# A two-layer decoder step on one core: the first pass of the output projection stores its split weight tiles, the second pass loads them back

## What is computed

```python
def gated_out(o, gate, w_o):
    return (o * jax.nn.silu(gate)) @ w_o

mp = gated_out(o.reshape(n_b, seq, MLA_WIDTH), gate, mla_w_o[l])   # 2048 -> 1024
hp = hp + rmsnorm(mp, post_norm[i])
```

## Time and profile before

| | us |
|---|---|
| median of 3 runs | 1649.53 |
| lowest and highest | 1646.85, 1650.47 |
| the profiled execution | 1646.13 |
| its span | 1644.3 |
| TensorE busy in the span | 1573.4 |
| second pass, from its first matmul to the next stage's first | 73.95 |

### The profile page before, as it was taken

The page is one execution under the profiler, slowest core; times in us unless marked ns, Lnnn a source line. Parts: engine busy times, 40 slices in busy tenths (PEclk is TensorE's granted clock), DMA queues, the critical chain, the costliest instruction groups (busy, mean ns, idle before and its releaser), DMA issues.

```text
span 1644.3 us, 27925 instructions
## 1 busy us (share of the span) xinstructions
PE 1573.4 (96%) x10778; PEld 1481.1 (90%) x10778; DVE 843.6 (51%) x1488; ACT 573.8 (35%) x1250; POOL 619.7 (38%) x683
## 2 busy tenths in 40 slices
PE   7999999899999999999999889999899999999996
PEld 7999999799999999999999668999899999977895
DVE  5227411675766757575756454006974430179416
ACT  4113111344444444444444343012232220289421
POOL 2433334133333333333332523456623324279610
PEclk9999999999999999999999999999999999999998
DMA  4122233011111111111115964227344223354223
GB/s 182 51 64 86 94 99 114 33 43 52 49 43 51 44 42 46 52 46 40 46 57 176 339 247 167 75 66 244 123 176 166 102 76 127 129 155 139 78 100 119
DMA packets 96077, 170.13 MB, mean 103 GB/s; under 512 B 9826, under 2 KB 63859, under 8 KB 95667
## 3 DMA queue, kind: packets, MB, share of 16 engines
q1 hardware_dynamic: 84372, 130.97, 24.4%
q10 hardware_dynamic: 6208, 21.26, 3.2%
q0 software_dynamic: 5376, 16.26, 2.7%
HBM read 129.04 MB, written 41.50 MB: 104 GB/s over the span
## 4 chain that ended last, share of the span: by engine, by line
PE 85%; DVE 9%; issue 3%; ACT 2%; POOL 1%; DMA 0%; DVEq 0%; SPq 0%; ACTq 0%; POOLq 0%
PE ps L128 27%; PE ps L987 8%; PE ps L2291 6%; PE ps L1054 6%; PE ps L2495 6%; PE ps L1038 4%; PE ps L993 3%; PE ps L1000 2%; PE ps L1018 2%; PE ps L1019 2%; PE ps L1020 2%; PE ps L1021 2%; PE ps L1022 2%; PE ps L2421 2%; PE ps L2897 1%
## 5 line engine op out<-in xcount | busy, mean ns | idle before, releaser
L683 POOL TENSOR_SCALAR b_prob<-b_prob,b_share 128x896 f32<-128x896 f32 (+7 forms) x128 | 97.3, 761 | 280.2 <-DVE b_share L903 278.9
L1946 POOL CAST w_hi_d<-w_raw_d 128x1024 fp32r<-128x1024 f32 x38 | 44.6, 1173 | 231.4 <-PE ps L128 109.3
L128 PE MATMUL ps<-a_xh,w_hi_a 128*128 128x344 f32 x552 | 119.6, 326 | 11.2 <-DVE a_xl L398 11.2
L781 ACT ACTIVATE b_pth<-ps 128x512 fp32r<-128x512 f32 (+1 forms) x160 | 86.2, 555 | 99.8 <-PE ps L1038 90.9
L128 PE MATMUL ps<-a_xl,w_hi_a 128*128 128x344 f32 x552 | 118.4, 323 | 0.0
L128 PE MATMUL ps<-a_xh,w_lo_a 128*128 128x344 f32 x552 | 118.0, 323 | 0.0
L773 ACT ACTIVATE b_prob<-ps,b_least 128x896 f32<-128x896 f32 (+7 forms) x128 | 94.8, 743 | 50.6 <-DVE b_least L895 49.5
L908 DVE TENSOR_TENSOR b_ptl<-ps,b_pth 128x512 fp32r<-128x512 f32 (+1 forms) x160 | 99.1, 632 | 24.7 <-ACT b_pth L781 23.6
L895 DVE TENSOR_REDUCE b_least<-ps 128x1 f32<-128x896 f32 (+7 forms) x128 | 96.2, 752 | 30.1 <-PE ps L1024 29.4
L128 PEld LDWEIGHTS ps<-a_xh,w_hi_a 128*128 128x128 f32 x552 | 94.2, 191 | 12.1 <-issue 11.6
L987 PE MATMUL ps<-cqh,b_w_hi 128*128 128x344 f32 x300 | 99.3, 331 | 0.2 <-DVE b_ql L835 0.2
(11 more groups left out here) (369 smaller groups left out, 4509.8 us busy)
## 6 DMA issues: line engine op xcount, KB each, us to landing
w_raw_d<-in_w_tiles SPq DMA_DIRECT2D x46, 512.0 KB, 3.6
c_pages<-in_cache_pages SPq DMA_DIRECT2D x80, 160.0 KB, 3.7
w_raw_a<-in_w_tiles SPq DMA_DIRECT2D x23, 512.0 KB, 3.5
gate_scratch<-a_stage ACTq DMA_DIRECT2D x16, 512.0 KB, 2.6
o_scratch<-b_ov POOLq DMA_DIRECT2D x64, 128.0 KB, 2.6
q_scratch<-f_qst ACTq DMA_DIRECT2D x16, 512.0 KB, 3.6
s_q<-q_scratch SPq DMA_DIRECT2D x32, 256.0 KB, 4.0
b_gate<-gate_scratch SPq DMA_DIRECT2D x60, 128.0 KB, 2.7
```

The lines of the kernel that those rows point to most:

```text
L128: mm = nc.tensor.matmul(ps[:, bank + c, 0:CH], wt, xt[:, k0 + k, c * CH:(c + 1) * CH], start=first and x == 0, stop=last and x == 2)
L683: nc.gpsimd.tensor_scalar(prob[:, n % 4, 0:keys], prob[:, n % 4, 0:keys], share[:, n % 4:n % 4 + 1], 1.0, ALU.mult, ALU.mult).then_inc(nor ...
L781: nc.scalar.activation(pth[:, n % 4, 0:cols], ps[:, 4 + n % 2, 0:cols], ACT.Copy).then_inc(pt_hi, 1)
```

## The change

After a tile of the first pass is split, SyncE stores its high and low part in a scratch tensor in HBM (`split_dram`, 16 tiles of 2 x 512 KB). The second pass loads the parts of its tiles from there (`load_again`) and splits nothing: neither GpSimd nor VectorE works on tiles 16 to 31. It uses four places, the fourth being the space of the two raw tiles (`of_raw`). The extra raw tiles `raw_more` are gone. The stores of tiles 0 and 1 are in `mla_samples`, behind the early heads' loads and the raw loads and ahead of `wv`. GpSimd now waits, before it writes over a split tile of the first pass, until that tile's store is complete (`split_kept`). The semaphores for stores and loads are ones that earlier loads of cache pages used, so counts start at a base.

```diff
@@ mla_samples, sync
         load_tile(nc, sp, w, a["w_tiles"], B_MO, 1, 0)
+        for u in range(2):
+            sp.wait_ge(w.split, u + 1)
+            for i, part in enumerate((w.hi, w.lo)):
+                nc.sync.dma_start(g.split_dram[1 - u, i], part[:, u, :].bitcast(F32)).then_inc(page_in[0][u], 16)
         sp.wait_ge(scored, ROUNDS * CHUNKS)
@@ out_and_swa_front
+    of_raw = at("w_of_raw_d", [P, 2, D], 66048, R32)
+    fourth = of_raw[:, 0, :], of_raw[:, 1, :]
-    raw_more = at("m_raw_more", [P, 2, D], 156672)
-    by_dve = [t for t in range(N_OUT, first_f) if t % 2]
-    slot = [(t - N_OUT + 2) % 3 if N_OUT <= t < first_f else t % 2 for t in range(n_tiles)]
+    slot = [t % 2 if t not in again else 2 if t == first_f - 1 else (2, 0, 1, 3)[t % 4] for t in range(n_tiles)]
...
+    def split_again(eng, t):
+
+        eng.wait_ge(split_in[slot[t]], split_in_base[slot[t]] + 32 * sum(slot[b] == slot[t] for b in range(N_OUT, t + 1)))
+
+    def split_kept(eng, t):
+
+        eng.wait_ge(split_out[t % 2], split_out_base[t % 2] + 32 * (t // 2 + 1))
@@ sync
+        def keep_split(t):
+            split_done(sp, t)
+            for i, part in enumerate(parts(t)):
+                nc.sync.dma_start(g.split_dram[t, i], part.bitcast(F32)).then_inc(split_out[t % 2], 16)
+
+        def load_again(t):
+            if slot_before[t] is not None:
+                sp.wait_ge(w.used, slot_before[t] + 1)
+                if slot_before[t] < N_OUT:
+                    split_kept(sp, slot_before[t])
+            elif slot[t] == 2:
+                sp.wait_ge(w.used, N_OUT - 1)
+            else:
+                split_done(sp, N_OUT - 1)
+            kept = t - N_OUT
+            split_kept(sp, 1 - kept if kept < 2 else kept)
+            for i, part in enumerate(parts(t)):
+                nc.sync.dma_start(part.bitcast(F32), shaped(g.split_dram[kept, i], t)).then_inc(split_in[slot[t]], 16)
+
+        for t in range(3, N_OUT):
             load(t)
-        sp.wait_ge(w.used, N_OUT)
+            keep_split(t - 1)
+        keep_split(N_OUT - 1)
+        for t in (N_OUT, N_OUT + 1, N_OUT + 3, N_OUT + 2):
+            load_again(t)
         for k in range(KT):
             nc.sync.dma_start(x_early[:, k, :], a["x_turned"][k][:, 0:SPLIT]).then_inc(x_early_in, 16)
-        for t in range(N_OUT + 3, N_OUT + 6):
-            load(t)
+        for t in range(N_OUT + 4, N_OUT + 8):
+            load_again(t)
         for k in range(KT):
             nc.sync.dma_start(x_late[:, k, :], a["x_turned"][k][:, SPLIT:TOK]).then_inc(x_late_in, 16)
-        for t in range(N_OUT + 6, first_f + 2):
-            load(t)
+        for t in range(N_OUT + 8, first_f - 4):
+            load_again(t)
+        for t in range(first_f - 4, first_f - 1):
+            load_again(t)
+        sp.wait_ge(w.used, first_f - 4)
+        load(first_f), load(first_f + 1)
+        load_again(first_f - 1)
@@ gpsimd
+                if t < N_OUT:
+                    split_kept(pool, t - 2)
...
-        for t in range(2, n_tiles):
+        for t in [t for t in range(2, n_tiles) if t not in again]:
@@ vector: the eight calls rest(17), rest(19), ... rest(31) are gone, for instance
-        rest(21)
         to_unit(0, 2), add_x(0, 2), x_low(0, 1)
@@ tensor, second pass
         for t in range(N_OUT, first_f):
             j = t // 2 - KT
-            split_done(pe, t)
+            split_again(pe, t)
```

More of the change, by code:

```diff
@@ L1682, in mla_samples @@
     p.sync, p.gpsimd, p.scalar, p.vector, p.tensor = sync, gpsimd, scalar, vector, tensor
+    p.pages_landed = [(landed, 16 * 4 * (QUAD - len(by_pool))) for landed, by_pool in zip(page_in[0], pool_share)]
     p.own_made, p.clear_queries, p.find_pages, p.load_query_weights = own_made, clear_queries, find_pages, load_query_weights
@@ L1852, in out_and_swa_front, with split_number, raw_before @@
     v_order = (NT,) + tuple(range(NT))
-    by_dve = [t for t in range(N_OUT, first_f) if t % 2]
+    again = range(N_OUT, first_f)
     v_tiles = (n_tiles - 2, n_tiles - 1)
[L1855 to L1858, removed]
-    slot = [(t - N_OUT + 2) % 3 if N_OUT <= t < first_f else t % 2 for t in range(n_tiles)]
+    slot = [t % 2 if t not in again else 2 if t == first_f - 1 else (2, 0, 1, 3)[t % 4] for t in range(n_tiles)]
     slot_before = [max((b for b in range(t) if slot[b] == slot[t] and b not in v_tiles), default=None) for t in range(n_tiles)]
-    def raw_tile(t):
-        return w.raw[:, raw_slot[t], :] if raw_slot[t] < 2 else raw_more[:, raw_slot[t] - 2, :]
+    def split_number(t):
+        return t + 1 if t < N_OUT else t + 1 - N_OUT
+    def raw_before(t):
+        return t - 2 if t != first_f and t != first_f + 1 else t - 2 - N_OUT
     def parts(t):
@@ L1871, in parts @@
             return w.hi[:, slot[t], :], w.lo[:, slot[t], :]
-        return third
+        return third if slot[t] == 2 else fourth
     def parts_of(t, k):
@@ L1889, in split_done @@
     def split_done(eng, t):
[L1891 to L1894, removed]
+        eng.wait_ge(w.split, split_number(t))
+    def split_again(eng, t):
+        eng.wait_ge(split_in[slot[t]], split_in_base[slot[t]] + 32 * sum(slot[b] == slot[t] for b in range(N_OUT, t + 1)))
+    def split_kept(eng, t):
+        eng.wait_ge(split_out[t % 2], split_out_base[t % 2] + 32 * (t // 2 + 1))
     def sync(sp, swa_samples):
@@ L1898, in load @@
             n = t - first_f
[L1899 to L1903, removed]
+            tile = B_MO + t if t < first_f else B_SIN + (n if n < NQ + 2 else n + 2 if t not in v_tiles else n - NQ)
@@ new lines, in load @@
+            split_done(sp, raw_before(t))
+            nc.sync.dma_start(w.raw[:, t % 2, :], a["w_tiles"][tile]).then_inc(w.landed[t % 2], 16)
+        def keep_split(t):
[15 more added lines that the diff above has]
+                nc.sync.dma_start(part.bitcast(F32), shaped(g.split_dram[kept, i], t)).then_inc(split_in[slot[t]], 16)
@@ L1938, in split @@
             hi, lo = parts(t)
-            pool.wait_ge(landed[raw_slot[t]], 16 * raw_count[t])
+            pool.wait_ge(w.landed[t % 2], 16 * ((t if t < N_OUT else t - N_OUT) // 2 + 1))
             if t in v_tiles:
@@ L1944, in split @@
             else:
[L1945 to L1949, removed]
-        for t in range(2, n_tiles):
+                pool.wait_ge(w.used, slot_before[t] + 1)
+                if t < N_OUT:
+                    split_kept(pool, t - 2)
+            nc.gpsimd.tensor_copy(hi, w.raw[:, t % 2, :]).then_inc(w.rounded, 1)
+            pool.wait_ge(w.rounded, split_number(t))
+            nc.gpsimd.tensor_tensor(lo, w.raw[:, t % 2, :], hi.bitcast(F32), ALU.subtract).then_inc(w.split, 1)
+        for t in [t for t in range(2, n_tiles) if t not in again]:
             if t == clear_at:
@@ L2147, in add_late @@
                                     ALU.add).then_inc(summed_late, 1)
-        def rest(t):
-            hi, lo = parts(t)
-            dve.wait_ge(w.rounded, t + 1)
-            nc.vector.tensor_tensor(lo, shaped(raw_tile(t), t), hi.bitcast(F32), ALU.subtract).then_inc(split_dve, 1)
         def spaces(of, to, n, root_sem, root_no, inv_sem, space_sem):
```

11 lines of the change are left out of this document (3 added, 8 removed).

## The result

The changed kernel takes 1638.83 us (median of 11 runs, 1633.98 to 1640.19), the kernel before, measured beside it, 1646.85 us (11 runs, 1642.11 to 1650.47). The ratio is 0.994, with a 95% interval of 0.993 to 0.9951: 8 to 11.5 us less. The forecast was 1639 and -10.2 us. The profiled execution took 1640.03 us for a span of 1638.3.

A forecast was written before the change was run, and what follows sets the result against it. TensorE bounds the kernel, held up in the second pass by VectorE's late splits; -10.9 - 0.3 + 1.0 = -10.2 us, from a median of 1649.53 to 1639. Gain range 7 to 13 us; 8 in 10 between 1634 and 1647.

The forecast's parts named there:

- -10.9 in the second pass: Second pass of the output projection: 73.95 us would fall to 63.0 once tiles 16 to 31 need no splitting.
- first two parts: Second pass's lost 10.9 us: about 5.2 are TensorE's waits for late low parts, 3.1 half speed after them.
- The remaining 2.6 are many waits of a few tenths: Second pass: the last 2.6 of the 10.9 us lost were put down to short TensorE waits at tile starts.
- VectorE left with 44 us, 37 without the slowdown: Second pass: VectorE's 64.25 us less 20 for eight subtractions leaves at most 44, 7 less without mutual slowdown.
- they lengthen each other's work: Second pass: VectorE and GpSimd slow each other; a low part takes 0.93 us with GpSimd resting, else 1.85.
- Neither can be late on its own account.: Second pass: without the splits, VectorE and ScalarE (21 us) are both paced by TensorE.
- -0.3 behind the pass: Behind the second pass: the second column sum no longer waits for VectorE's last additions, gaining 0.3 us.
- +1.0 for the DMA: Second pass: reload waits, likeliest at tiles 20 and 24, put between 0 and 2.9 us and taken as 1.
- The stores: 32 stores of 512 KB: cost 0 in the first pass; those of tiles 0 and 1 at most 1 us.
- 352 GB/s: Rival 1, second pass: reload at this rate instead of 407, gain 5.3 to 8.3 us, about 1642.5; chance 0.16.
- Rival 2: Second pass: third place loads at only 154 GB/s, 6.8 us a tile; net +5 us, 1654.5; chance 0.06.
- Rival 3: No change: VectorE or ScalarE sets the pace, or store waits cost the first pass; 1648 to 1650; chance 0.08.

## Why the prediction was right

- **-10.9 in the second pass.** Measured -10.46 (73.95 to 63.49), and -10.2 to -10.5 in the part that all profiles share. The target was 63.0; the missing 0.5 is no wait of TensorE (0.04 us). Less 2.6 us for the column sums and the spreading, its 384 matmuls took 60.9 us, 0.159 each where 0.157 was taken. What makes them that much longer than in the first pass stays open. The reading of what was lost was right in its first two parts only. "The remaining 2.6 are many waits of a few tenths" is wrong: besides the three waits named, the profile has two, of 0.30 and 0.18 us, and TensorE was idle 5.8 us in all (73.95 less 68.14). Some 2 us were busy time at a slower pace outside the two stretches at half speed. Most of them went too, and no run shows why.
- **VectorE left with 44 us, 37 without the slowdown.** Measured 31.35. The eight subtractions had taken 17.4 us, not the 20 that three of them suggested, so the same sum would have given 46.8; that 44.12 came out so near to 44 when GpSimd alone was loaded is in part luck. The step "they lengthen each other's work" was right in kind and too small: the residual additions fall from 1.38 to 0.88 us too, and the sums of the late chunk from 1.24 to 0.61, not the low parts alone.
- **"Neither can be late on its own account."** Right for this kernel: VectorE's eight subtractions, at 7/8 of their size, could be put back without a cost once GpSimd rested, and the other way round.
- **-0.3 behind the pass.** Measured -0.4 to -1.3 from the sums to the next stage, in the changed kernel's three profiles against the first of before, -0.8 in the mean. What was forecast itself came out: from the eight-matmul sum to the second column sum it is 2.79 us in all three, against 3.07, so -0.3. The other 0.5 lies further back and scatters with the clock: the stretch took 41.2 us at a granted clock of 1.00 and 41.7 and 42.1 at 0.96.
- **+1.0 for the DMA.** Measured 0.3 to 0.4 us on a weight load in five profiles, and 0.2 to 0.5 of TensorE in three others (at tile 20 twice, at tile 16 once), at most 0.7 us of the pass. So this term and the one above, -9.9 together, measured -10.46. The forecast had tile 20 land 17.0 us after the first matmul of the pass and be wanted at 17.8; it landed at 18.0 (1134.68 less 1116.69). Of the 407 GB/s taken for it, 401 came from 1120 to 1126 us, with the residual in the queue, and 383, 6% less, from 1118 to 1132. Tile 24 was not waited for. The narrow fit was real: with one place less, tile 19 is late by 2.5 us.
- **The residual at VectorE.** Forecast 1128.5, 13.4 us into the pass; it was there at 1131.3, 14.6 us in, 1.2 us later. Nothing hung on it.
- **The stores.** In the first pass 0, as said. Tiles 0 and 1: "cost 0, at most 1" rested on the transfer of `wv` being the one in the way. It was another, the raw load of tile 0, ahead of the stores in the queue; it costs GpSimd 1.4 us and the time perhaps 0.6. The mechanism was missed; that its size fell into the bound is luck.
- **The sum.** -10.46 - 0.8 + 0.6 is -10.7, against -10.2 forecast and 8 to 11.5 measured. That 1638.83 lies 0.2 us from the 1639 forecast is luck: the forecast set out from a median of 1649.53 over three runs, and before's median beside the changed kernel was 1646.85, so the two medians differ by 8.0 us (9.9 by the ratio). The single profile gives -6.0 between the spans, since before's was at the good end of the draw in its rest (412.7) and after's was not.
- **The rivals.** The reload did not run at 352 GB/s at the place that decided: while the residual moved it was about 400. The mean of the whole pass, 356 GB/s at a DMA share of 1.01, is the bytes of the pass over the time that TensorE, which never stood still for more than 0.04 us, needed for them. Rival 2's 154 GB/s for the third place is out, as tile 16 (issued at 1109.31) was never late by more than 0.2 us. Rival 3 is out with TensorE's 0.04 us of idle time in the pass, and with a first pass of 105.93 us against 105.94. The Trainium skill, "DMA: Bandwidth & Descriptors", "Where 436 GB/s comes from", has about 358 GB/s as the bound between HBM and SBUF; at 401 over six microseconds in this pass the trace does not agree. The same page, section "Measured", gives about 358 GB/s for each of two cores of an HBM domain that both stream, and this program runs on one core.

## What to carry to other kernels

Where data are prepared twice, storing the prepared form and loading it back can pay where the DMA engines have room (a share of 0.23 in the first pass and 0.52 in the second, before): here 17 MB written and 8 MB more read bought 10 us. Take the work off the engine that slows the critical one, not only off the critical one: VectorE was late only with both loads together, and taking off GpSimd's half alone would have done as much as taking off its own. Count the room for prefetch in microseconds of queue, large foreign transfers included: the fourth place looked like a reserve and carried two thirds of the gain.

## What the runs showed of the hardware

- VectorE's low part of 688 columns, all in SBUF, took 0.93 us with GpSimd at rest and 1.63 to 1.85 in the mean with it working, on the weight tiles or on spare memory; the addition of two SBUF tiles 0.88, and 0.97 to 1.38. The same size with one operand in PSUM (`mt<-ps,mt`) took 0.86 to 0.87 in all of them. GpSimd's copies of 896 columns took 1.16 us beside VectorE's own work and 1.37 with the subtractions added.
- Half speed after a wait of TensorE was the same for two causes: 21 matmuls took 5.01 us after 2.10 us for VectorE and after 2.50 for a DMA. After waits of 0.43 and 0.74 us for a DMA, in the run with both splits put back, the next 18 took 2.97 us and the next 21 took 3.47, full speed; after 1.06 us, with three places, the granted clock stayed at 1.00 too.
- The issue of a tile's two loads to the third place took SyncE 1.33 us at 1109.31 and 5.78 at 1122.07, behind the residual's 2.8 MB. The engine is then held in the issue, and the profile names no wait.
- 1 MB of stores, issued 3.5 us behind a 512 KB load on the same queue that was still on its way, made GpSimd get that load's tile 1.4 us later (four profiles without them, nine with, and no overlap).
